# Two hybrid blocks on one core: the second up unit of the second MLP chunk in seven products

## The reference, cut to what matters

```
D_MODEL, SEQ, D_FF = 1024, 512, 4096
def sq_relu_mlp(h, w_up, w_down):                 # h: (512, 1024)
    return jnp.square(jax.nn.relu(h @ w_up)) @ w_down
# in each of the two layers (i = 0, 1):
f = sq_relu_mlp(rmsnorm_2(x, g[2]), w_mlp_up[i], w_mlp_down[i])
x = x + rmsnorm_2(f, g[3])
```

## Time and profile before

| | |
|---|---|
| median of three runs | 1710.83 us (1710.01 to 1711.23) |
| the profiled execution | 1711.5 us, of which 1709.7 us are the span of the trace |
| busy in the span: PE, DVE, ACT | 1688.6 us (99%), 1272.5 us (74%), 957.2 us (56%) |
| mean granted TensorE clock | 0.997 of full speed |
| the chain of work that ended last | PE 88%, DVE 8%, ACT 3% of the span |

### The profile page before, as it was taken

The page is one execution under the profiler, slowest core; times in us unless marked ns, Lnnn a source line. Parts: engine busy times, 40 slices in busy tenths (PEclk is TensorE's granted clock), DMA queues, the critical chain, the costliest instruction groups (busy, mean ns, idle before and its releaser), DMA issues.

```text
span 1709.7 us, 25289 instructions
## 1 busy us (share of the span) xinstructions
PE 1688.6 (99%) x9375; PEld 1459.4 (85%) x9375; DVE 1272.5 (74%) x2020; ACT 957.2 (56%) x1645; POOL 169.8 (10%) x147
## 2 busy tenths in 40 slices
PE   9999999999999999999999999999999999999998
PEld 7888877888788897789899988878887999999977
DVE  6378877776567776589698986775566978898966
ACT  4267875665436666478556364652235866464655
POOL 2011212000300000220000002320003000000041
PEclk9999999999999999999999999999999999999999
DMA  8222124214243222243232433313322432323621
GB/s 270 84 73 74 40 73 101 75 50 148 75 110 76 74 75 81 74 173 117 81 121 81 145 152 132 99 62 103 114 91 87 161 123 99 99 99 100 234 75 50
DMA packets 152786, 177.52 MB, mean 104 GB/s; under 512 B 18281, under 2 KB 126342, under 8 KB 150886
## 3 DMA queue, kind: packets, MB, share of 16 engines
q1 hardware_dynamic: 150790, 159.22, 29.8%
q10 hardware_dynamic: 1888, 16.85, 2.5%
HBM read 158.82 MB, written 12.58 MB: 100 GB/s over the span
## 4 chain that ended last, share of the span: by engine, by line
PE 88%; DVE 8%; ACT 3%; issue 1%; DMA 1%; DVEq 0%; SPq 0%; ACTq 0%
PE bank L1158 27%; PE bank L1159 26%; PE bank L1160 26%; PE bank L1507 2%; DVE split_weights L2671 2%; PE bank L1531 1%; PE bank L1426 1%; DVE act_b L2671 1%; PE bank L1415 1%; DMA raw_weights<-in_w_mlp_down 1%; DVE act_a L2673 0%; PE bank L1823 0%; ACT act_a L1920 0%; DVE work L2706 0%; PE bank L1341 0%
## 5 line engine op out<-in xcount | busy, mean ns | idle before, releaser
L1158 PE MATMUL bank<-act_a,split_weights 128*128 128x512 f32 (+1 forms) x1360 | 525.4, 386 | 6.3 <-DVE act_a L2671 2.0
L1160 PE MATMUL bank<-act_a,split_weights 128*128 128x512 f32 (+1 forms) x1360 | 518.8, 381 | 0.0
L1159 PE MATMUL bank<-act_a,split_weights 128*128 128x512 f32 (+1 forms) x1360 | 518.1, 381 | 0.0
L1158 PEld LDWEIGHTS bank<-act_a,split_weights 128*128 128x128 f32 x1360 | 256.0, 188 | 58.5 <-issue 6.1
L1160 PEld LDWEIGHTS bank<-act_a,split_weights 128*128 128x128 f32 x1360 | 255.6, 188 | 50.3
L1159 PEld LDWEIGHTS bank<-act_a,split_weights 128*128 128x128 f32 x1360 | 256.0, 188 | 45.1 <-issue 0.2
L1158 PE MATMUL bank<-act_b,split_weights 128*128 128x256 f32 (+1 forms) x648 | 207.4, 320 | 0.3 <-DVE split_weights L3355 0.2
L1160 PE MATMUL bank<-act_b,split_weights 128*128 128x256 f32 (+1 forms) x648 | 206.4, 318 | 0.0
L1159 PE MATMUL bank<-act_b,split_weights 128*128 128x256 f32 (+1 forms) x648 | 206.3, 318 | 0.0
L2613 DVE TENSOR_TENSOR split_weights<-raw_weights,split_weights 128x2048 fp32r<-128x2048 f32 x55 | 127.1, 2311 | 76.1 <-ACT split_weights L1865 63.3
L1865 ACT ACTIVATE split_weights<-raw_weights 128x2048 fp32r<-128x2048 f32 x51 | 97.3, 1908 | 119.5 <-PE bank L1160 119.5
(11 more groups left out here) (356 smaller groups left out, 3261.5 us busy)
## 6 DMA issues: line engine op xcount, KB each, us to landing
raw_weights<-in_w_mlp_up SPq DMA_DIRECT2D x32, 1024.0 KB, 5.4
raw_weights<-in_w_mlp_down SPq DMA_DIRECT2D x32, 1024.0 KB, 5.3
raw_weights<-in_w_in SPq DMA_DIRECT2D x18, 1024.0 KB, 5.3
raw_weights<-in_w_conv_in SPq DMA_DIRECT2D x12, 1024.0 KB, 5.2
raw_weights<-in_w_attn_in SPq DMA_DIRECT2D x16, 512.0 KB, 5.3
raw_weights<-in_w_ple_gate SPq DMA_DIRECT2D x8, 1024.0 KB, 5.1
raw_weights<-in_w_out SPq DMA_DIRECT2D x4, 1024.0 KB, 5.1
raw_weights<-in_w_attn_in SPq DMA_DIRECT2D x4, 1024.0 KB, 5.4
```

What stands on the lines that cost most here:

```text
L1158: nc.tensor.matmul(dst, w[0], a[0], start=first, stop=False)
L1159: nc.tensor.matmul(dst, w[0], a[1], start=False, stop=False)
L1160: mm = nc.tensor.matmul(dst, w[1], a[0], start=False, stop=last)
```

## The change

Unit 9, the second up unit of chunk 1, is done in seven products as well, in both layers. It takes four PSUM banks (2, 3, 4, 5) in the place of two, and is no longer split at the end of chunk 0 (`n2 n3` are taken out there); its parts `g7` to `g13`, sums, mixes and copy come into the strings of chunk 1. Of the plain unit 11 that follows, the halves `N6` and `N7` stood side by side after the hidden tile of unit 9; now `N6` stands ahead of that tile and `N7` within it. The last unit of the MLP counts its tiles by two more, so that the count of tiles stays the same for what follows; it computes and waits for nothing else.

```diff
-PRODUCT_UPS = ((), (2,), (0, 2), (2,))
+PRODUCT_UPS = ((), (1, 2), (0, 2), (2,))
+LAST_TILES = 4 + 2 * (sum(len(ups) for ups in PRODUCT_UPS) % 2)
...
-        return 2 if j < 4 and j not in PRODUCT_UPS[c] else 4 if (c, j) == (LAST, 7) else 0
+        return 2 if j < 4 and j not in PRODUCT_UPS[c] else LAST_TILES if (c, j) == (LAST, 7) else 0
...
-UP_BANKS = (((0, 1), (2, 3), (4, 5), (6, 7)), ((0, 1), (2, 3), (6, 7, 0, 1), (4, 5)),
+UP_BANKS = (((0, 1), (2, 3), (4, 5), (6, 7)), ((0, 1), (2, 3, 4, 5), (6, 7, 0, 1), (4, 5)),
...
-                   "p27 a7 n0 a8 a9 n1 a10 H3 n2 a11 a12 a13 n3",
+                   "p27 a7 n0 a8 a9 n1 a10 H3 a11 a12 a13",
+                   "g7 g8 g9 g10 g11 s0 b0 g12 t0 v0 g13 g14 o1 g15 g16 g17 g18 g19 g20 N6 o2 s1 b1 N7 t1 v1 p0 "
...
+                   "G1 g7 g8 g9 g10 F1 g11 T0 b0 y0 g12 t0 v0 g13 G2 g14 g15 d4 d5 g16 g17 F2 d6 d7 g18 g19 g20 N6 T1 b1 N7 y1 t1 v1 "
...
-            def three(dst, w, a, first, last, done=None):
+            def three(dst, w, a, first, last, done=None, count=1):
...
-                    mm.then_inc(done, 1)
+                    mm.then_inc(done, count)
...
-                              part == k == 0, part == 1 and k == 3, done)
+                              part == k == 0, part == 1 and k == 3, done,
+                              LAST_TILES - 3 if part and (k, m) == (3, 3) else 1)
...
-                    V.tensor_tensor(out_, in_halves(last_banks(name)[m][:, :]), out_, ALU.add).then_inc(tile_read, 1)
+                    V.tensor_tensor(out_, in_halves(last_banks(name)[m][:, :]), out_, ALU.add)\
+                        .then_inc(tile_read, LAST_TILES - 3 if m == 3 else 1)
```

More of the change, by code:

```diff
@@ L770, in hybrid_block_kernel @@
                    "p14 p15 X2 a0 p16 a1 p17 H2 a2 p18 a3 p19 a4 p20 a5 p21 a6 p22 p23 X3 p24 p25 p26 "
-                   "p27 a7 n0 a8 a9 n1 a10 H3 n2 a11 a12 a13 n3",
-                   ACT_THIRD + "p14 p15 p16 p17 p18 p19 p20 p21 p22 p23 p24 p25 p26 p27 i0 i1 i2 i3",
[2 rows of a table added]
+                   + ACT_THIRD[ACT_THIRD.index("p1 p2"):] + "p14 p15 p16 p17 p18 p19 p20 p21 p22 p23 p24 p25 p26 p27 i0 i1 i2 i3",
                    "i4 i5 i6 o0 N2 N3 " + ACT_THIRD + "p14 p15 p16 p17 p18 p19 p20 p21 p22 p23 p24 p25 p26 p27 n0 n1 n2 n3",
@@ L778, in hybrid_block_kernel @@
         DVE_MLP = ("T0 b0 y0 t0 v0 U3 T1 b1 y1 t1 v1 S0 p0 p1 p2 z0 p3 T2 b2 y2 t2 v2 Q0 p4 p5 H0 p6 S1 p7 T3 b3 y3 p8 t3 p9 v3 z1 "
-                   "Q1 p10 p11 H1 p12 p13 S2 p14 p15 Q2 p16 z2 p17 p18 H2 p19 p20 S3 p21 p22 p23 z3 p24 p25 p26 p27 n0 Q3 n1 H3 n2 n3",
-                   "G2 " + DVE_THIRD + DVE_DOWN + "I0 a7 i0 a8 i1 i2 a9 i3 K0",
+                   "Q1 p10 p11 H1 p12 p13 S2 p14 p15 Q2 p16 z2 p17 p18 H2 p19 p20 S3 p21 p22 p23 z3 p24 p25 p26 p27 n0 Q3 n1 H3",
+                   "G1 g7 g8 g9 g10 F1 g11 T0 b0 y0 g12 t0 v0 g13 G2 g14 g15 d4 d5 g16 g17 F2 d6 d7 g18 g19 g20 N6 T1 b1 N7 y1 t1 v1 "
+                   + DVE_THIRD[DVE_THIRD.index("d8"):] + DVE_DOWN + "I0 a7 i0 a8 i1 i2 a9 i3 K0",
                    "A10 i4 i5 i6 A11 A12 d0 N2 d1 d2 N3 A13 G2 d3 " + DVE_THIRD + DVE_DOWN + "n0 a7 a8 n1 a9 a10 n2 a11 a12 n3 a13",
```

## The result

The changed kernel takes 1712.98 us (median of 20 runs, 1712.35 to 1713.94), the kernel before 1710.95 beside it: 2.03 us more, ratio 1.0013 with a 95% interval of 1.0007 to 1.0019. The forecast was 1713.1. Run again later it took 1713.27 against 1711.02, ratio 1.0012 (1.0003 to 1.0021).

A forecast was written before the change was run, and what follows sets the result against it. PE was taken as the bound, busy 1688.6 of 1709.7 us. Waits of 2.01 us less 0.88 saved give 1.13 per layer, 2.26 in all: 1710.83 + 2.26 = 1713.1 us; 8-in-10 range 1709.0 to 1715.2.

The forecast's parts named there:

- The chain: Layer 0, units 9 to 11: `F2` ends at 835.12, `N7` on DVE at 842.82, unit 11 effectively starts at 842.98.
- the hand-overs: Some ten passes from engine to engine in the sum, up to 0.1 us each; range 1.0 below, 1.2 above.
- The sum of 1.13 us per layer: Unit 11 starts 1.13 us later than before: waits of 2.01 us, of which the saving pays 0.88.
- PE's saving: Unit 9 on PE, 10.88 to 10.00 us: 0.88 us less per layer, 1.76 us over two layers.
- rival A: Weights are in time, so only PE's 1.76 us saving counts: 1709.1 us; chance 0.14.
- B: PE's clock halves after the wait ahead of unit 11, 1.71 us each time: 1714.8 or 1716.5 us; chance 0.13.
- C: DVE's lag grows past 4.0 us, PE waits in unit 13, some 1 us per layer: 1715.1 us; chance 0.05.

The follow-up runs named there:

- e5: Changed kernel with `G2` and `N7` earlier, and unit 9's mixes `d6 d7` and tile steps `o2 s1 T1` moved forward too; 1708.96 us, ratio 0.9988.
- e7: Changed kernel with `F2` between `d6` and `d7` on DVE; 1713.00 us, ratio 1.0008.
- e4: Changed kernel with `F2` behind the mixes `d6` and `d7` on DVE; 1717.95 us, ratio 1.0037.
- e6: Changed kernel with `N6` and `N7` again behind the whole hidden tile of unit 9, as before the change; 1722.37 us, ratio 1.0066.
- e1: Changed kernel with `N7` moved ahead of the hidden tile of unit 9, behind `o2` on ACT and `N6` on DVE; 1713.28 us, ratio 1.0008.
- e2: Changed kernel with `g12` and the sums of unit 10 (`G2`) earlier, right behind `g11` on DVE; 1712.02 us, ratio 1.0004.
- e3: Changed kernel with `G2` early and `N7` between `s1` and `b1` on ACT, between `T1` and `b1` on DVE; 1710.57 us, ratio 0.9994.
- e9: As e1, but unit 12's three sums on DVE made on 64 of 512 columns, the rest left out; 1709.89 us, ratio 0.9996.
- e10: Changed kernel in its own order, with unit 12's three sums made on 64 of 512 columns; 1713.07 us, ratio 1.0014.
- e8: The changed kernel run again without any edit; 1713.27 us, ratio 1.0012.

## Why the prediction was right

**The chain, link by link.** Counted from unit 9's start, forecast and then measured in layer 0: `T0` starts at 2.93 and 2.94; `g14` ends at 10.24 and 10.24; `F2` ends at 14.15 and 14.17; `N7` starts on ACT at 19.54 and 19.53 and ends on DVE at 21.85 and 21.83; unit 11's effective start 22.01 and 22.00 (second matmul 842.26 less one pitch of 0.23). The durations of the trace before carried over to the new order nearly unchanged, and the hand-overs, for which 1.0 us below and 1.2 above was allowed over two layers, came out as taken. Unit 10's effective start (its second matmul's less one pitch) is 10.40 us after unit 9's, as forecast: its first matmul stands 0.06 behind the end of `g14`, at 10.30, and its second follows 0.22 later in the place of 0.12. The sum of 1.13 us per layer measured 1.15 and 1.11. The runs show 2.03 for 2.26, which lies within the interval of the ratio (1.2 to 3.3 us).

**PE's saving.** 0.88 us per layer was a little too much. Without any wait (e5) units 9 to 11 take 31.01 us against 31.79: 0.78. Two units in products in a row ran at 10.06 and 10.04 in the place of the 10.00 of the earlier trace rows. The forecast did not hang on it, since its sum sets the start of unit 11 by the end of `N7`; only rival A's 1.76 us did.

**The rivals.** A (in time) is what e5 shows: there `N7` ends 19.73 us after unit 9's start, 0.37 ahead of unit 11; in the changed order it ends 2.1 us later. B (the clock) didn't happen at 1.49 us of wait, nor at 1.62 (e7), and did at 2.34 and 4 (e4, e6). It was a fair rival with nearly the right price: 1.6 us for 1.71 in three of these four stalls, 2.6 in the fourth. The row it took for its 2.04 us of idle PE was not a sure sign, as the last section shows.
The Trainium skill's page "TensorE: Matmul & The Clock Gate", section "The HAM clock gate", has an idle array fall back to half its clock. The first 4 us behind the waits of 2.34 and 4 us agree (0.59 and 0.50 on average, in e4 and e6); behind 1.49 and 1.62 us the granted clock stayed at 1.00.

**What was wrong in it.** C put DVE's margin at 1.8 us, in unit 13's fourth part, a part of the weights. That part's lead was indeed 1.90 in the trace after (864.70 + 0.69 on DVE, 867.29 on PE):

```profile
864.70 1.48 DVE L2675 TENSOR_TENSOR split_weights<-sums,split_weights 128x512 fp32r<-128x512 f32 x2
...
867.29 0.29 PE L1161 MATMUL bank<-act_b,split_weights 128*128 128x256 f32 x1
```

But the margin lies elsewhere, at the banks, and is smaller. DVE's last additions of the chunk, in the changed kernel and in e1:

```profile
894.32 1.28 DVE L3370 TENSOR_TENSOR work<-bank,work 128x512 f32<-128x512 f32 x2
```

```profile
896.40 1.28 DVE L3370 TENSOR_TENSOR work<-bank,work 128x512 f32<-128x512 f32 x2
```

Counted from unit 9's start (820.03 and 821.30), they stand 0.8 us later in e1, with unit 12 coming 1.64 us sooner (31.30 in the place of 32.94), which is 2.4 together, and PE waits 1.5 for banks; so by this count some 0.9 us were left, not 1.8. It didn't touch the forecast, but it would have spoiled the obvious remedy: "move `N7` forward" takes away the wait that the profile names, and gives back nothing. DVE is busy for 69.05 us of units 9 to 15 after the change (24.41 + 39.64 = 64.05 before), where PE needs 71.1. Two engines are nearly full there. DVE's idle time in the stretch, behind its first step and up to its last one of the chunk, is 3.1 us in the changed kernel, 3.9 in e1, 2.4 in e2, 2.5 in e3 and 1.8 in e5, the fastest. But that sum does not decide by itself: e2 has no more of it than e3 and is slower, with its `N7` later (21.22 against 20.38 us after unit 9's start), and e9 has e1's 3.9 and takes 1.3 us less in each layer's stretch.

## What to carry to other kernels

A wait that one engine's profile names can be removed and come back elsewhere when the engine that feeds it has no idle time left behind that place, as in e1. So add up that engine's busy time over the whole stretch first; what helped here was to close its gaps as well (e5), and not to move the late step alone. A saving of 0.8 us per layer on the busiest engine ended as 2 us won (e5), 2 us lost (the changed kernel) or 11 us lost (e6), by nothing but the order of the steps on two other engines.

## What the runs showed of the hardware

PE's clock after a stall, with the waits counted as above: ten waits of 1.2 to 1.62 us at unit 11 (changed kernel and its repeat, e2, e7, e10, two layers each), and none of them was followed by a lower clock; four of 2.34 us and above there (e4, e6) all were, at 1.6 us or more each. The profile's idle time for them is 1.0 to 1.5 and 2.2 to 3.8 us. The stall near 666 us lies between, with 2.03 us of idle time (2.3 us from one matmul's start to the next one's) in all twelve traces and the same instructions ahead of it. The clock fell behind it in five (before, e1, e3, e8, e9) and not in seven (the changed kernel's first, e2, e4 to e7, e10). So one profile does not tell whether a stall of that length costs its own time alone or some 1.6 us more (the 23 matmuls from its end on take 5.27 us in e8 and 3.66 in the changed kernel's first profile). Why it differs between executions is open.
